# Sums of the latents' tiles on GpSimd in three transitions of a two-block transformer kernel, and four activated condition rows at other places

## The reference, cut to what matters

```python
def ffn_sublayer(x, shift, scale, gate, w_in, w_out, ln_g, ln_b):
    y = swiglu_2(modulate_2(x, shift, scale), w_in, w_out)
    return layer_norm(ALPHA * x + 0.5 * gate * y, ln_g, ln_b)

def layer_norm(x, g, b):
    mu = jnp.mean(xf, axis=-1, keepdims=True)
    var = jnp.mean(jnp.square(xf - mu), axis=-1, keepdims=True)
    return ((xf - mu) * lax.rsqrt(var + LN_EPS) * g + b).astype(x.dtype)

def modulation(cond, w_mod, b_mod):
    m = jax.nn.silu(cond) @ w_mod + b_mod
    return jnp.split(m[..., None, :], N_MOD, axis=-1)
```

## Time and profile before

| | |
|---|---|
| median of 3 runs | 2569.63 us (2568.29 to 2571.73) |
| profiled execution | 2564.72 us, of it span 2562.9 us |
| TensorE busy | 2461.3 us, 96% |
| weight loads busy | 2234.7 us, 87% |
| VectorE busy | 1854.6 us, 72% |
| ScalarE busy | 1107.6 us, 43% |
| GpSimd busy | 0.2 us |
| mean granted TensorE clock | 0.987 |

### The profile page before, as it was taken

The page is one execution under the profiler, slowest core; times in us unless marked ns, Lnnn a source line. Parts: engine busy times, 40 slices in busy tenths (PEclk is TensorE's granted clock), DMA queues, the critical chain, the costliest instruction groups (busy, mean ns, idle before and its releaser), DMA issues.

```text
span 2562.9 us, 39610 instructions
## 1 busy us (share of the span) xinstructions
PE 2461.3 (96%) x15670; PEld 2234.7 (87%) x15670; DVE 1854.6 (72%) x3605; ACT 1107.6 (43%) x1658; POOL 0.2 (0%) x4
## 2 busy tenths in 40 slices
PE   4999999999999999999999999999999999998998
PEld 3998989999999888788888998888998888877998
DVE  7878988878878736768787669896785444676655
ACT  3444565444463324634232652232642322645444
POOL 0000000000000000000000000000000000000000
PEclk8999999999999999999999999999999999999999
DMA  8886766758867531654443256675373333212653
GB/s 314 304 268 221 255 216 228 259 194 270 292 203 224 179 99 59 214 160 129 139 147 121 87 190 209 193 236 198 95 259 125 114 107 96 83 58 75 198 191 105
DMA packets 161961, 455.80 MB, mean 178 GB/s; under 512 B 17776, under 2 KB 21360, under 8 KB 161776
## 3 DMA queue, kind: packets, MB, share of 16 engines
q1 hardware_dynamic: 161776, 453.26, 54.2%
HBM read 452.14 MB, written 1.05 MB: 177 GB/s over the span
## 4 chain that ended last, share of the span: by engine, by line
PE 77%; DVE 5%; ACT 2%; issue 1%; DMA 1%; ACTq 0%; DVEq 0%; SPq 0%
PE PS L1189 24%; PE PS L1190 24%; PE PS L1191 24%; DVE own L1678 1%; PE PS L1216 1%; PE PS L1343 1%; PE PS L1214 1%; DVE X L1659 1%; ACT own L1408 1%; PE PS L1389 1%; PE PS L1372 0%; DMA SCR<-in_ma 0%; ACT Uh L1469 0%; ACT NT L1473 0%; PE PS L1317 0%
## 5 line engine op out<-in xcount | busy, mean ns | idle before, releaser
L1189 PE MATMUL PS<-Uh,own 128*128 128x256 f32 (+1 forms) x2072 | 656.1, 317 | 41.5 <-DVE Ul L1759 21.3
L1190 PE MATMUL PS<-Ul,own 128*128 128x256 f32 (+1 forms) x2072 | 645.2, 311 | 0.0
L1191 PE MATMUL PS<-Uh,own 128*128 128x256 f32 (+1 forms) x2072 | 645.1, 311 | 0.0
L1408 ACT ACTIVATE own<-raw 128x1024 fp32r<-128x1024 f32 x429 | 448.2, 1054 | 374.3 <-PE PS L1191 305.8
L1678 DVE TENSOR_TENSOR own<-raw,own 128x1024 fp32r<-128x1024 f32 x429 | 520.1, 1219 | 70.3 <-ACT own L1408 70.1
L1189 PEld LDWEIGHTS PS<-Uh,own 128*128 128x128 f32 x2072 | 398.9, 193 | 70.6 <-issue 31.8
L1190 PEld LDWEIGHTS PS<-Ul,own 128*128 128x128 f32 x2072 | 400.0, 193 | 19.5 <-issue 0.2
L1191 PEld LDWEIGHTS PS<-Uh,own 128*128 128x128 f32 x2072 | 399.7, 193 | 19.7
L1189 PE MATMUL PS<-Hh,own 128*128 128x256 f32 (+1 forms) x1096 | 347.7, 317 | 1.0 <-DVE own L1678 0.6
L1190 PE MATMUL PS<-Hl,own 128*128 128x256 f32 (+1 forms) x1096 | 343.2, 313 | 0.0
L1191 PE MATMUL PS<-Hh,own 128*128 128x256 f32 (+1 forms) x1096 | 343.2, 313 | 0.0
(11 more groups left out here) (216 smaller groups left out, 3883.9 us busy)
## 6 DMA issues: line engine op xcount, KB each, us to landing
MODS<-in_mm SPq DMA_DIRECT2D x168, 256.0 KB, 3.5
SCR<-in_mm SPq DMA_DIRECT2D x136, 256.0 KB, 3.7
raw<-in_f0i SPq DMA_DIRECT2D x68, 512.0 KB, 4.2
raw<-in_f1i SPq DMA_DIRECT2D x56, 512.0 KB, 3.6
raw<-in_f2i SPq DMA_DIRECT2D x56, 512.0 KB, 3.6
SCR<-in_ma SPq DMA_DIRECT2D x88, 256.0 KB, 5.5
raw<-in_w1i SPq DMA_DIRECT2D x44, 512.0 KB, 4.8
raw<-in_w2i SPq DMA_DIRECT2D x44, 512.0 KB, 4.6
```

Source lines behind the costliest of these rows:

```text
L1189: e.matmul(o, ll, rh, start=start, stop=False)
L1190: e.matmul(o, lh, rl, start=False, stop=False)
L1191: return e.matmul(o, lh, rh, start=False, stop=stop)
L1408: e.activation(parts(w.n)[0], raw[:, w.n % RING, :], ACT.Copy).then_inc(s["whi"].tell(w.n), 1)
```

## The change

The latents' tiles k = 0 to 5 at the end of f0, go and f1 are added up by GpSimd: for k = 1 to 5 an add of X and an add of the squares, into NT's half for the latents. The steps carry a mark, pool. TensorE's pairs then are three (the sum, k = 6, k = 7), and because the limit is BEHIND + 1 in this case, all three stand behind the one context chunk. f2 keeps folded = 0. The adds wait for what was in NT: for f0 and f1 until an earlier norm has read it (ulo of nf and l01), for go until the middle modulation steps are through, since row 3 lies there.

Condition rows 3 and 4 are activated, and the middle modulation steps allowed, two chunks later, in block 2 of the value part. Rows 5 and 6 are loaded where they were, but activated inside the latents' f1 input part, behind its second gate and up (four steps of early(LAT)).

```diff
-    def square(self, t, k, folded=FOLDED):
+    def square(self, t, k, folded=FOLDED, pool=False):
+        t["pool"] = pool
...
-        if len(t["todo"]) > BEHIND:
+        if len(t["todo"]) > (BEHIND + 1 if pool else BEHIND):
             self.sums(t)
...
         for i in range(j - n + 1, j + 1):
-            self.freed[i] = ("folded", (t["n"], k, "q"))
+            self.freed[i] = ("pool_folded" if t["pool"] else "folded", (t["n"], k, "q"))
...
-                self.square(self.tallies[q], mm, 0 if r is LAT and st in ("f0", "go", "f1", "f2") else FOLDED)
+                self.square(self.tallies[q], mm, 0 if r is LAT and st == "f2" else FOLDED,
+                            r is LAT and st in ("f0", "go", "f1"))
...
-    for who in (1, 2):
-        p.put("cond", q=who, n=2 + who)
-    p.mod_limit = MIDDLE * 16
-    p.rate = 2.0
     for blk in range(2, 6):
-        p.drain(gv(blk, (0, 1, 2, 3)))
+        both = gv(blk, (0, 1, 2, 3))
+        if blk == 2:
+            next(both)
+            next(both)
+            for who in (1, 2):
+                p.put("cond", q=who, n=2 + who)
+            p.mod_limit = MIDDLE * 16
+            p.rate = 2.0
+        p.drain(both)
...
     for who in (1, 2):
         p.put("condload", q=who, n=4 + who)
-        p.put("cond", q=who, n=4 + who)
+    def conditions():
+        for who in (1, 2):
+            p.put("cond", q=who, n=4 + who)
...
-        p.drain(early(LAT))
+        latents = early(LAT)
+        if conditions:
+            for _ in range(4):
+                next(latents)
+            conditions()
+        p.drain(latents)
...
-                        on.wait_ge(s["folded"], (w.n, w.k, "q"))
+                        on.wait_ge(s["pool_folded" if w.pool else "folded"], (w.n, w.k, "q"))
...
+        def gpsimd(e):
+            on = Queue(e)
+            nt_read = {"f0": ("nf", KT - 1), "f1": ("l01", KT - 1)}
+            for w in plan.order:
+                lo, hi = w.r
+                if w.what == "fold" and w.pool:
+                    x, q = NT[:, lo // S, 0, :], NT[:, lo // S, 1, :]
+                    st = w.after[1][0]
+                    if w.k == 1:
+                        x0, q0 = X[:, 0, lo:hi], SQ[:, (w.j - 1) % 4, :]
+                        if st == "go":
+                            on.wait_ge(s["modded"], last_middle_mod)
+                        else:
+                            on.wait_ge(s["ulo"], nt_read[st])
+                    else:
+                        x0, q0 = x, q
+                        on.wait_ge(s["pool_folded"], (w.n, w.k - 1, "q"))
+                    on.wait_ge(s["acc"], w.after[1])
+                    e.tensor_tensor(x, x0, X[:, w.k, lo:hi], ALU.add).then_inc(s["pool_folded"].tell((w.n, w.k, "x")), 1)
+                    on.wait_ge(s["squared"], w.j)
+                    e.tensor_tensor(q, q0, SQ[:, w.j % 4, :], ALU.add).then_inc(s["pool_folded"].tell((w.n, w.k, "q")), 1)
```

More of the change, by code:

```diff
@@ L137 @@
     eps: float = 0.0
+    pool: bool = False
 class Plan:
@@ L337, in fold @@
         for i in range(j - n + 1, j + 1):
-            self.freed[i] = ("folded", (t["n"], k, "q"))
-        self.put("fold", n=t["n"], k=k, r=t["r"], j=j, centred=t["centred"], after=t["before"](k))
+            self.freed[i] = ("pool_folded" if t["pool"] else "folded", (t["n"], k, "q"))
+        self.put("fold", n=t["n"], k=k, r=t["r"], j=j, centred=t["centred"], after=t["before"](k), pool=t["pool"])
         if last:
@@ L348, in sums @@
         self.put("sums", n=t["n"], k=k, r=t["r"], j=-1 if j is None else j, bank=t["bank"], centred=t["centred"],
-                 first=t["first"], final=k == KT - 1)
+                 first=t["first"], final=k == KT - 1, pool=t["pool"])
         t["first"] = False
@@ L818, in schedule, with between @@
         p.put("condload", q=who, n=4 + who)
-        p.put("cond", q=who, n=4 + who)
-    def between(sites, l, i, ll, sec, st, g, before, then):
+    def conditions():
+        for who in (1, 2):
+            p.put("cond", q=who, n=4 + who)
+    def between(sites, l, i, ll, sec, st, g, before, then, conditions=None):
         kept, p.rate = p.rate, 0.0
@@ L851, in schedule @@
     p.rate = 3.2
-    between(("l01", "c01"), 0, 1, 0, 6, "f1", 8, "gu", {1: reopen})
+    between(("l01", "c01"), 0, 1, 0, 6, "f1", 8, "gu", {1: reopen}, conditions)
     p.rate = 3.2
@@ L978 @@
     "pooled", "roped1", "mapped", "y_lo", "masked", "weight1", "merged", "m_lo", "v_part", "v_stat", "v_normed", "mixed",
-    "sq_sum", "root_inv", "spreads", "head_x", "roped2", "weight2", "o_lo", "final_x")
+    "sq_sum", "root_inv", "spreads", "head_x", "roped2", "weight2", "o_lo", "final_x",
+    "pool_folded")
 def build(nc, T, out, plan, known):
@@ L1716, in vector @@
                                                op1=ALU.mult).then_inc(s["coef"].tell(key), 1)
-                elif w.what == "fold":
+                elif w.what == "fold" and not w.pool:
                     ax, aq = NT[:, lo // S, 0, :], NT[:, lo // S, 1, :]
@@ L2009, in vector @@
                     e.tensor_tensor(x, x, RS[:, 0, 0, :], ALU.mult).then_inc(s["final_x"].tell(w.k), 1)
+        def gpsimd(e):
[19 more added lines that the diff above has]
+                    e.tensor_tensor(q, q0, SQ[:, w.j % 4, :], ALU.add).then_inc(s["pool_folded"].tell((w.n, w.k, "q")), 1)
         with nc.Block() as block:
+            block.gpsimd(gpsimd)
             block.tensor(tensor)
```

## The result

The changed kernel takes **2572.9 us** (median of 18 runs) against 2568.32 us of the kernel before (18 runs): ratio 1.0018, 95% interval 1.0011 to 1.0024, so **4.6 us slower** (2.8 to 6.2). The forecast was 1.3 us faster. The time lies in the upper half of the stated range, but on the other side of no change.

What follows compares the result with a forecast made beforehand. TensorE was busy 96%, but at the transitions its queue and the context's norm chain ran neck and neck. Gains 2.0 + 1.0 + 1.9 = 4.9 us less 3.6 for GpSimd's hold-up gave 2569.63 - 1.3 = 2568.3 us, range 2561 to 2577.

Steps and rivals of the forecast that it cites:

- the walk: Both engines of the context's norm followed through the transitions: last Ul 2.8 us sooner in C, 1.9 us in B.
- Sum before any cost of GpSimd: Gain over the three transitions without GpSimd's cost: 2.0 + 1.0 + 1.9 = 4.9 us.
- A: Transition from feed-forward f0 to the gated MLP; predicted gain 2.0 us, bounds 1.0 and 4.26.
- C: Transition from f1 to f2; last Ul 2.8 us sooner, less 0.9 for one more pair: gain 1.9 us.
- B: Transition from go to f1; last Ul 1.9 us sooner, less 0.9 for one more pair: gain 1.0 us.
- from 0.7 and 2.3 us to some 3 to 5: Expected sign: TensorE's wait for Ul ahead of the context chunk grows from 0.7 (C) and 2.3 us (B).
- What they do to VectorE: GpSimd's adds delay VectorE's two-operand passes in the norm: 2.4 us halved to 1.2 us a transition, 3.6 in all.
- The rows cost 1.9 us of B's chain: At B, ScalarE's two condition rows and table loads delay the mean: lag 2.51 us against 0.63 in C.
- Rival 1: VectorE isn't held up by GpSimd at all: 4.9 us less, 2564.8 us; chance 0.23.
- Rival 2: TensorE's removed time counts in full: 12.8 us less, 2556.8 us; half of it 2563.2; chance 0.12.
- Rival 4: GpSimd's adds are too long, so TensorE gets the k = 5 sum late: 2578 us; chance 0.05.
- Rival 3: VectorE's hold-up in the context's norm, 3.4 to 6.8 us per transition: 5.3 to 15.5 us slower; chance 0.15.

Runs made afterwards that it cites:

- e3: The changed kernel without GpSimd's adds, the sum of tiles 0 to 5 left out of the mean; ratio 0.9993 to the kernel before.
- e5: The changed kernel with unread matmuls of ones in TensorE's first-chunk waits, 9 in A, 22 in B, 7 in C; ratio 1.0004 to the kernel before.
- e4: The changed kernel with unread matmuls of ones in TensorE's first-chunk waits, 9 in A, 11 in B, 7 in C; ratio 1.0010 to the kernel before.
- e1: The kernel before with only the condition rows moved, no GpSimd adds, TensorE's eight pairs kept; ratio 1.0002 to the kernel before.
- e2: The changed kernel with the condition rows back at their old places, GpSimd's adds and three pairs kept; ratio 1.0021 to the kernel before.
- e10: As e9 with three tiles on GpSimd and 10 unread matmuls in B, 3 in C; 2564.06 us against 2567.94, ratio 0.9986.
- e8: The changed kernel with only tiles 0 and 1 added on GpSimd, the other six with a pair each; ratio 0.9999 to the kernel before.
- e9: As e8 with 7 unread matmuls of ones ahead of f1's first context chunk; ratio 0.9995 to the kernel before.

## Why the prediction was wrong

**Right: what bounds, and the walk.** That a pair costs 0.85 us, that TensorE's time alone is worth little, that the waits ahead of the chunk would grow and L1659's would go: all as read. "Sum before any cost of GpSimd", 4.9 us, is e3 with 4.2 by the lengths, A and C within 0.15 us, B short by its fallen clock. The same sum from the other side: e5, with the clock kept, is 0.8 us slower with 5.8 us of hold-up, which leaves 5.0.

**The step that failed: the wait was priced at its own length.** The prediction let TensorE's wait grow, "from 0.7 and 2.3 us to some 3 to 5", and had no term for the clock behind it. Rows at 0.5 of the clock showed that such a wait is followed by work at half speed: 3.9 us in B and C (e5), more than the error of any term that the sum had. The page's strip of the granted clock and the 1.00 in all transitions before could have raised the question: what keeps it there, if TensorE is to idle longer? TensorE: Matmul & The Clock Gate of the Trainium skill, Part 1, says that recent activity decides between 2.4 and 1.2 GHz; e4 and e5 agree.

**Second: "What they do to VectorE" was mis-sized.** Taken 1.2 us a transition, measured 1.8, 1.8 and 2.2, so 5.8 in place of 3.6. The halving for VectorE's idle time was the fault: where TensorE no longer paces it, hardly any of the delay is absorbed. The full 2.4 us by the mean rest of an add was nearer. A pass that the list of two-operand passes left out, L1723 over 128x8, took 0.55 us of it in B. This alone turns the forecast from 1.3 us faster to 0.9 slower (5.8 - 4.9); e5 measured 0.8. The clock makes the rest of the 4.7.

**Third: B, right in its sum and wrong in its parts.** "The rows cost 1.9 us of B's chain" holds only where TensorE's pairs are gone. With eight pairs e1 gives 0.0: VectorE waited 0.8 us for TensorE because it was late, and without the lag waits 2.5 us. Without the pairs it holds the last Ul up by 1.84 us (e2 against after). The walk put both edits into one and could not tell them apart, but its end was right: 1.9 us predicted, 1.96 measured in e3. That B became 0.2 us shorter there and not 1.0 is the clock.

**A held a wait that was not in the prediction.** "TensorE is not stopped by the chain at once" is wrong: the changed kernel waits 3.67 us in A's first chunk, in the timeline of TensorE:

```profile
1016.72 0.67 PE L1205 MATMUL PS<-own,Ul 128*128 128x512 f32 x1 [3.67 <-DVE X L1760]
```

L1760 is the centring, the last reader of the context's mean in its PSUM bank, and the plan gives that bank (3) to the chunk's second half. It cost nothing in the end, since "A gives what the context chain gives" held.

**The rivals.** Rival 1 is out (Ul at 0.93 us). Rival 2 is out: e3, without any hold-up, saved 4.2 of the 12.8 us. Rival 4 is out: the adds ended in time everywhere; only e10 ever waited for one. Rival 3, the hold-up in the gain's place, has the mechanism right and decides where it said, from 1.6 us per transition on; at the measured 1.8 to 2.2 it gives only the 0.9 us, and 3.9 us of the 4.7 are the clock's.

## What to carry to other kernels

Work taken off the busiest engine is worth what the next chain gives back, and where the busiest engine is TensorE its new wait can cost twice: once as idle time, once as the half-speed work behind it. Ask of each edit that lengthens a TensorE wait whether the granted clock survives it, and keep it busy there, with useful work moved in or, as a test, with matmuls nobody reads. An idle GpSimd is no free engine beside VectorE passes with two SBUF operands: place its adds beside passes that read PSUM or a single operand.

## What the runs showed of the hardware

- GpSimd adds two 128x256 float32 tiles in 0.74 us undisturbed (VectorE 0.42), up to 1.27 us where it meets a VectorE pass with two SBUF operands; VectorE's passes rose from 0.42 to 0.95 us at most, and one over 128x8 from 0.17 to 0.73. In the rows shown it is the one that started second.
- The clock fell though no single wait was long: in C at 1829.3 us, behind waits of 0.45, 1.39 and 0.70 us (a fourth, 0.75, came later). In e8 it fell with the waits that e1 had without a fall (1.54, 0.36, 0.36 us). What decides between such cases was not settled; both may differ in when the waits came, which no run varied alone.
- Matmuls of ones with ones of 128 columns, 0.22 us each, kept it at 1.00 where they filled the waits (e5, e9). Whether fewer would do was not tried.
